# A compression stage with two heads per transposition, 64-row products and sums folded outside TensorE

## The reference, cut to what matters

```python
def compress(rows, lw):                       # rows: B, N, 2 (k or v), 4 heads, 64
    R = L_CMP // D_CMP                        # 32 // 16 = 2
    chunks = rows.reshape(B, N // D_CMP, D_CMP, 2, N_KV, HEAD_DIM)
    w1 = lw['phi_w1'].reshape(2, L_CMP, HEAD_DIM, PHI_HIDDEN)
    part = jnp.einsum('bcjehd,esjdf->bcsehf', chunks, w1.reshape(2, R, D_CMP, HEAD_DIM, PHI_HIDDEN))
    n_blk = N // D_CMP - R + 1
    pe_term = jnp.einsum('ejd,ejdf->ef', lw['phi_pe'], w1)[:, None, :]
    h = sum(part[:, s:s + n_blk, s] for s in range(R)) + pe_term
    return jnp.einsum('bcehf,efd->bcehd', jax.nn.silu(h), lw['phi_w2'])
```

## Time and profile before

| | |
|---|---|
| the profiled execution | 4675.83 us, span 4674.2 us |
| busy share of the span | TensorE 84%, its weight loads 76%, VectorE 36%, ScalarE 23%, GpSimd 8% |
| mean granted TensorE clock | 0.866 of full speed |
| the compression stage | from 1429.7 us (first DMA issue) to 1912.2 us (first instruction of the next stage) |
| its first and last steps | first transposition 1465.07 us, last product of the steps 1902.04 us |

### The profile page before, as it was taken

One profiled execution on the slowest core, in us unless ns is written; L12 is line 12 of the kernel. 1 busy time (PEld: TensorE's weight loads), 2 busy tenths in 40 slices (PEclk: granted clock), 3 DMA queues, 4 the chain that ended last, 5 costly groups with the idle time before them and its releaser, 6 DMA issues. The chain is left out here.

```text
span 4674.2 us, 75290 instructions
## 1 busy us (share of the span) xinstructions
PE 3911.9 (84%) x31650; PEld 3558.5 (76%) x31650; DVE 1672.6 (36%) x2048; ACT 1086.5 (23%) x1480; POOL 356.8 (8%) x459
## 2 busy tenths in 40 slices
PE   4999994477754888897984978979999999999997
PEld 3999992366643766565982538979999999999997
DVE  4222217733255777221001553233333233332235
ACT  1111103333223555120001422121111211211210
POOL 1000002333310000000001330000000000000000
PEclk8999985677777999796555788989999999999998
DMA  3333313422104432362543014132233332233332
GB/s 101 112 111 111 100 37 98 123 73 75 46 19 172 168 148 112 94 199 78 153 124 140 10 45 126 54 91 84 89 91 91 91 91 86 87 92 90 91 91 82
DMA packets 538916, 452.85 MB, mean 97 GB/s; under 512 B 110044, under 2 KB 497259, under 8 KB 533643
## 3 DMA queue, kind: packets, MB, share of 16 engines
q1 hardware_dynamic: 508546, 323.84, 24.3%
q0 software_dynamic: 11696, 108.55, 6.0%
q10 hardware_dynamic: 18432, 16.79, 1.2%
HBM read 414.92 MB, written 45.75 MB: 99 GB/s over the span
## 5 line engine op out<-in xcount | busy, mean ns | idle before, releaser
L2477 DVE TENSOR_TENSOR f_w_lo<-f_w,f_w_hi 128x2048 fp32r<-128x2048 f32 x132 | 302.6, 2292 | 955.9 <-ACT f_w_hi L2455 955.9
L53 PE MATMUL f_ps<-hh,f_w_hi 128*128 128x260 f32 x2816 | 569.7, 283 | 62.6 <-DVE f_w_lo L2477 37.9
L57 PE MATMUL f_ps<-hh,f_w_lo 128*128 128x260 f32 x2816 | 569.7, 284 | 0.0
L55 PE MATMUL f_ps<-hl,f_w_hi 128*128 128x260 f32 x2816 | 569.0, 284 | 0.0
L2455 ACT CAST f_w_hi<-f_w 128x2048 fp32r<-128x2048 f32 x132 | 252.0, 1909 | 1062.1 <-DMA f_w<-in_w_gate 433.4
L53 PEld LDWEIGHTS f_ps<-hh,f_w_hi 128*128 128x128 f32 x2816 | 436.6, 189 | 65.5 <-DVE f_w_lo L2477 38.3
L57 PEld LDWEIGHTS f_ps<-hh,f_w_lo 128*128 128x128 f32 x2816 | 436.3, 189 | 0.0
L55 PEld LDWEIGHTS f_ps<-hl,f_w_hi 128*128 128x128 f32 x2816 | 435.0, 189 | 0.0
L53 PE MATMUL f_ps<-f_hid_hi,f_w_hi 128*128 128x260 f32 x1408 | 284.4, 283 | 6.7 <-DVE xt L2496 6.7
L57 PE MATMUL f_ps<-f_hid_hi,f_w_lo 128*128 128x260 f32 x1408 | 283.5, 283 | 0.0
L55 PE MATMUL f_ps<-f_hid_lo,f_w_hi 128*128 128x260 f32 x1408 | 282.6, 282 | 0.0
(11 more groups left out here) (426 smaller groups left out, 6737.8 us busy)
## 6 DMA issues: line engine op xcount, KB each, us to landing
b_kbuf<-in_cache_slc_kv SPq DMA_DIRECT2D x384, 128.0 KB, 2.1
p_w<-in_w_in SPq DMA_DIRECT2D x46, 1024.0 KB, 5.6
f_w<-in_w_gate SPq DMA_DIRECT2D x44, 1024.0 KB, 5.7
f_w<-in_w_up SPq DMA_DIRECT2D x44, 1024.0 KB, 5.6
f_w<-in_w_down SPq DMA_DIRECT2D x44, 1024.0 KB, 5.1
b_kbuf<-in_cache_slc_kv ACTq DMA_DIRECT2D x128, 128.0 KB, 2.2
o_w<-in_w_o SPq DMA_DIRECT2D x16, 1024.0 KB, 5.9
rk_chunks<-r_outb POOLq DMA_DIRECT2D x8, 1280.0 KB, 5.7
```

Source lines behind the costliest of these rows:

```text
L53: pe.matmul(out[j], w_hi, x_hi[j], start=start, stop=False)
L55: pe.matmul(out[j], w_hi, x_lo[j], start=False, stop=False)
L57: last = pe.matmul(out[j], w_lo, x_hi[j], start=False, stop=stop)
L2477: dve.tensor_tensor(w_lo[:, s, :], w_raw[:, s, :], w_hi[:, s, :].bitcast(F32), ALU.subtract).then_inc(lo_done, 1)
```

## The change

`stage_compress` is written anew as a lane (one generator for each engine, unrolled, no hardware loops), run by `run_lanes`. What it does differently:

- A load takes 8 rows of 128 chunks instead of 16; there are three slots. No copy reorders the rows. A transposition takes one row j of two neighbouring heads as they lie in the slot, so the transposed tile has two heads in its two halves of 64 partitions and one row j.
- A step (`turn`, `mult`) is still four transpositions and 512 columns: two rows j times two head pairs, for keys or values. Keys and values alternate step by step, 16 steps for each half of a sample, 272 steps in all.
- A step's multiplication has 12 products of 64 rows and 256 columns instead of three of 128 rows and 512 columns: three precision terms, two rows j, two halves a of the partitions. The half a = 0 sums into bank 2, a = 1 into bank 3; keys and values take the two halves of a bank's columns.
- The transposed tiles go through two banks instead of four; the second-weight products use the same two, so the stage uses 4 banks in place of 8. `tb` has three buffers in place of four.
- After the 16 steps of a half, ScalarE copies the s = 1 partitions of both sum banks into `sh` (four copies of 64 x 256) and VectorE adds the s = 0 partitions with the shift (four additions of 64 x 256). The first product of the next half waits until both banks are free (`acc_free`). The product with `fold_r` and the splitting of sums are gone.
- The first weights lie twice in SBUF (once for each half of the partitions), in the third load slot, and their split operations have 4096 columns in place of 2048.
- `kc` and `vc` are no longer kept in SBUF: the stage writes them to HBM sample by sample, and `stage_nsa_sample` reads both back with two more DMAs, for which its first VectorE operation waits.

In the diff, `ends(n)` gives the half whose last step was n - 3, and nothing at other steps.

```diff
+    RING, TB = 3, 3
...
+    kv = sb("kv", [P, RING, 8, 512])
...
+    ps = ctx.enter_context(nc.psum_tensor("m_ps", [P, 4, 512], F32))
...
+    def tensor(pe):
...
+        def turn(n):
+            m, q, e = n // 16, n % 16 // 2, n % 2
...
+            ev = event(n)
+            if ev >= 2:
+                pe.wait_ge(dve_ev, ev - 1)
+            for j in range(2):
+                for hp in range(2):
+                    at = 2 * j + hp
+                    last = pe.transpose(ps[:, ev % 2, at * w:(at + 1) * w],
+                                        kv[0:w, load % RING, 2 * (q % 4) + j, e * 256 + hp * P:e * 256 + (hp + 1) * P],
+                                        g.ident[0:w, 0:w])
+            last.then_inc(turned, 1)
+        def mult(n):
...
+            pe.wait_ge(dve_ev, event(n) + 1)
+            if q == 0 and e == 0 and m:
+                pe.wait_ge(acc_free, 2 * m)
+            for k, (wt, x) in enumerate(((w1_hi, tb_hi), (w1_hi, tb_lo), (w1_lo, tb_hi))):
+                for j in range(2):
+                    for a in range(2):
+                        rows = slice(a * C, (a + 1) * C)
+                        last = pe.matmul(ps[:, 2 + a, 2 * e * w:2 * (e + 1) * w], wt[rows, e, 2 * q + j, :],
+                                         x[rows, n % TB, 2 * j * w:2 * (j + 1) * w], start=q == 0 and e == 0 and k == 0 and j == 0,
+                                         stop=q == JP - 1 and e == 1 and k == 2 and j == 1, skip_group_check=True)
+            last.then_inc(mm_done, 1)
...
+        for n in range(END + 1):
+            yield n
+            if n < NU:
+                turn(n)
+            if n in fin_at:
+                finish(n)
+            if 0 <= n - 2 < NU:
+                mult(n - 2)
+    def scalar(act):
...
+                act.copy(tb_hi[:, n % TB, 0:w], ps[:, event(n) % 2, 0:w]).then_inc(act_ev, 1)
+            m = ends(n)
+            if m is not None:
...
+                act.wait_ge(mm_done, n - 2)
+                for a in range(2):
+                    got = ps[C:P, 2 + a, 0:4 * w].rearrange("p (e q c) -> p e q c", e=2, q=2)
+                    for e in range(2):
...
+                            last = act.copy(sh_a[:, a, e, :, 127:255], got[:, e])
...
+                    last.then_inc(sh_copied, 1)
+    def vector(dve):
...
+                dve.tensor_tensor(tb_lo[:, n % TB, 0:w], ps[:, event(n) % 2, 0:w], tb_hi[:, n % TB, 0:w].bitcast(F32),
+                                  ALU.subtract).then_inc(dve_ev, 1)
...
+                for a in range(2):
+                    got = ps[0:C, 2 + a, 0:4 * w].rearrange("p (e q c) -> p e q c", e=2, q=2)
+                    dve.wait_ge(sh_copied, 2 * m + a + 1)
+                    for e in range(2):
+                        last = dve.tensor_tensor(sh_a[:, a, e, :, c0:c1], got[:, e, :, 0:c1 - c0], sh_a[:, a, e, :, c0:c1], ALU.add)
+                    last.then_inc(acc_free, 1)
...
 def stage_nsa_sample(nc, g):
+                    sp.dma_start(g.kc[:].rearrange("p (b q) c -> p b q c", b=NB), g.kc_samp.rearrange("b p q c -> p b q c")).then_inc(in_done, 16)
+                    sp.dma_start(g.vc[:], g.vc_samp.rearrange("b p n -> p b n")).then_inc(in_done, 16)
...
-                dve.wait_ge(in_done, 16 * 13)
+                dve.wait_ge(in_done, 16 * 15)
```

More of the change, by code:

```diff
@@ L1450, in stage_nsa_sample @@
+        run_lanes(nc, [compress(nc, g, ctx)])
 def stage_nsa_sample(nc, g):
@@ L2668, in nsa @@
 def nsa(nc, g):
+    stage_compress(nc, g)
     with ExitStack() as ctx:
@@ L2671, in nsa @@
         g.vc = ctx.enter_context(nc.sbuf_tensor("vc", [P, NB, 512], F32))
-        stage_compress(nc, g)
         stage_nsa_sample(nc, g)
@@ L2685, in build @@
     g.vc_prompt = nc.dram_tensor("vc_prompt", [31, 256], F32, kind="Internal").ap()
+    g.kc_samp = nc.dram_tensor("kc_samp", [NB, P, 2, 255], F32, kind="Internal").ap()
+    g.vc_samp = nc.dram_tensor("vc_samp", [NB, P, 512], F32, kind="Internal").ap()
     g.mix_t = nc.dram_tensor("mix_t", [D, TC], F32, kind="Internal").ap()
```

483 lines of the change are left out of this document (211 added, 272 removed).

## The result

The changed kernel takes 4752.1 us (median of 4 runs, 4748.0 to 4758.5), the kernel before 4672.2 (median of 4, 4665.6 to 4681.9): ratio 1.017, 95% interval 1.0147 to 1.0194, so 80 us slower. Predicted were 4765 us, 97 us more. The profiled execution of the changed kernel took 4750.74 us with a span of 4748.9; before, the span was 4674.2: 74.7 us more.

What follows compares the result with a forecast made beforehand. The compression stage was taken as bound by TensorE in order, and by VectorE where a half or group of 8 steps ends. Samples +78, start -2, prompt +5, detour +16: 4668 + 97 = 4765 us, range 4690 to 4850.

Steps and rivals of the forecast that it cites:

- Step: Compression stage: one step of transpositions (0.64 us) and products (0.91 us) takes 1.55 us instead of 1.14, bounds 1.40 and 1.75.
- no-drain rival: At switches, first weights load under the other kind's last product: step 1.15 us, total 4657 us; chance 0.13.
- Halves side by side: In a step's products, a pair costs what one costs, 0.118 us apart; rival without overlap 4947 us, chance 0.03.
- loads not waiting for their own half: In a step's products; the rival that they do wait made pairs 0.23 us, 4908 us in all, chance 0.04.
- Two banks cost nothing: Transposed tiles: the chain of a step, 2.1 us, fits in two steps, 3.1 us, with 1.0 us to spare.
- Fold: After each half, TensorE's next product waits 3.4 us, 16 times in the samples; bounds 2.0 and 4.5.
- Clock: In the samples, longer waits lower TensorE's clock: 1 us added a sample, bounds 0 and 6.
- Second-weight products: In each sample, these products take another 2.9 us, as in the kernel before.
- Sum of a sample: 32 x 1.55 + 2.9 + 2 x 3.4 + 1 = 60.3 us instead of 50.5, +78 us for eight.
- Start: Compression stage's start: 64 passes instead of 32, but a smaller first load and no first reordering copy; -2 us.
- prompt: Prompt's 16 steps at the lower clock level: some 2.4 us each, +5 us, bounds -8 and +10.
- Detour: Next stage's start: two 2 MB loads from HBM delay its first VectorE operation some 16 us; bounds +5 and +25.

Runs made afterwards that it cites:

- the kernel without changes: Changed kernel with six products of 128 rows in place of twelve of 64 rows, the two heads summed together: 4695.8 us (median of 5).

## Why the prediction was right

The total was 13 us too high, and the mechanism was the one forecast. By the steps:

- **Step, 1.55 predicted, 1.49 measured.** Products 0.91 us, as predicted. Transpositions to the first product 0.58 where I had 0.64: the 0.20 us from the last transposition to the next kind's first load came as forecast, but the exposed load ahead of the transpositions cost 0.055 us and not 0.11 (the second starts 0.164 us after the first, the others 0.109 apart). That each change of kind costs time was the deciding point, and the no-drain rival's 1.15 us is what the kernel without changes takes.
- **Halves side by side; loads not waiting for their own half.** Right: twelve products in 0.91 us. The rule of the Trainium skill, page "TensorE: Matmul & The Clock Gate", section "Part 3: Packing small matmuls — row/col tiling", that loads overlap only products of another row group did not hold here either.
- **Two banks cost nothing.** Right: in the samples of the changed kernel TensorE waits for VectorE's low part for 1.5 us in all, and also at steps of 1.15 us (no changes of kind) only seven times, behind silu, up to 1.4 us.
- **Fold, 3.4 predicted, 2.87 measured.** The bounds 2.0 and 4.5 held it; the durations of 0.37 and 0.41 us were as estimated, but the starts are 0.27 and 0.33 us apart where I added 0.40 and 0.45. To the first product the half costs 2.94 us.
- **Clock, +1 us a sample, 3.9 measured.** This term was mis-sized: 1.5 to 2.9 us went in slow steps behind each of the fifteen waits in the samples, 2.0 on average. I had the bounds (0 and 6), but took the low end since the kernel before waited too and had 0.97. There the waits of a sample were of 0.8 to 2.0 us; here TensorE stands still for 2.87 us after each half, and the granted clock is 0.50, its 1.2 GHz level, for the next one to three steps.
- **Second-weight products, 2.9, and silu.** Right: 2.9 us in a sample (1.1 and 1.8, by how much longer the two steps with them are). Silu stands in front of a copy on ScalarE for 1.14 us twice, which the chain's slack covers in the changed kernel but for one wait of 0.83 us. With two sum sets 0.8 us of it come out in each sample.
- **Sum of a sample.** 47.7 + 2.9 + 5.9 + 3.9 = 60.4 us, and I had 49.6 + 2.9 + 6.8 + 1 = 60.3. The near equality is luck: errors of -1.9, 0, -0.9 and +2.9. The eight came to +73 and not +78: the first took 54.8 us, as it has no second-weight products and only one wait for the fold (the sixteenth, 2.55 us, lies in the prompt's stretch), and the eight before took 405.4 us, not 404.
- **Start, -2 predicted, +1 measured; prompt, +5 and +5.8.** The 64 passes took 13.8 us. A prompt step took 1.98 instead of 2.4 us, so the prompt's right total is partly luck: the sixteenth wait for the fold lies in it.
- **Detour, 16 predicted.** Right in its total (16.8, and 16.6 when taken away), wrong in its place: 10.7 us at the query scaling and the rest later in that stage, where no run shows why, so the right total is partly luck. The scaling starts 13.9 us after the first of the two loads is issued, where two loads of 8.8 us one behind the other would take 17.6; so they overlap in part.
- **What was not in the prediction:** the FFN, -18 us. It accounts for the difference between the 97 us of the terms and the measured 75 to 80, with the 3.4 us by which the profile before reached this stage later.

## What to carry to other kernels

A pair of changes between operations of 128 and of 64 rows cost 0.34 us here at full clock, so operations of one kind are worth grouping: 1.49, 1.33, 1.24 us a step with changes at every step, every second and every fourth, which needs banks and buffers for a group, not faster engines. A wait of TensorE is to be priced with the low clock that may follow it (2.9 us became 4.9 on average in the changed kernel; in the run without changes of kind it followed only eight of fifteen), and a second set of sum banks removed both where the engines that fold had slack. When a stage that no one touched changes its length, look at TensorE's waits put down to "issue" at the same product of each round of a loop before looking for data: the place of the loop's code was worth up to 75 us in that stage here. It is the total that counts, though: the added products that took 20 us off the FFN took nothing off the kernel in its one run.

## What was unexpected of the hardware

- The same FFN loop, 11 rounds with the same data, took 1553 to 1629 us by the number of instructions ahead of it: 1553.4 (48 calls added), 1573.7 and 1574.7 (none), 1628.7 (16). Wherever the second stall stood, it ended 5.0 to 6.1 us after the first product of its round.
- Stops of TensorE of 2.87 us were each followed by 1.5 to 2.9 us lost at a granted clock of 0.50 in the changed kernel, and by none after seven of fifteen such stops in the run without changes of kind; after stops of 2.43 us the low clock came in about half of the cases. The Trainium skill, page "TensorE: Matmul & The Clock Gate", section "A second HAM failure mode: psum-queue depth-cycling", describes a kernel whose small idle stretches between groups of products make the clock go back and forth, at a cost paid between bursts; the windows of the changed kernel show such a back and forth, 1.00, 0.50, 1.00 within 36 us, though behind single stops of 2.87 us.
